# A diffusion-transformer block with a 16-expert MoE: both low parts of the first expert's w2 earlier on VectorE, w1's high parts laid out anew, overflow sums on GpSimd

## The reference

```python
h2 = rms_norm(x, norm2_g[layer]) * (1 + sc2) + sh2
...
scores = jax.nn.sigmoid(jnp.dot(h.astype(F32), router_w.astype(F32)))
biased = scores + router_b.astype(F32)
grp = biased.reshape(h.shape[0], N_EXPERT_GROUPS, EXPERTS_PER_GROUP)
grp_score = jnp.sum(lax.top_k(grp, TOP_K)[0], axis=-1)
best = jnp.argmax(grp_score, axis=-1)
...
for e in range(N_EXPERTS):
    he = jax.nn.silu(h @ w1[e]) * (h @ w3[e])
    y = y + gates[:, e:e + 1] * (he @ w2[e]).astype(F32)
...
x = x + g2 * f[:b * n].reshape(b, n, d)
...
return rms_norm(x, final_g)
```

## Time and profile before

| | us |
|---|---|
| median of 3 runs | 578.73 (577.07 to 579.29) |
| the profiled execution | 576.75 |
| its span | 574.2 |
| TensorE busy | 540.2 (94%) |
| VectorE busy | 445.2 (78%) |
| ScalarE busy | 322.2 (56%) |
| GpSimd busy | 159.4 (28%) |

### The profile page before, as it was taken

How to read it: one execution, slowest core, us unless ns; L and a number is a source line. 1 busy time by engine, 2 the same in 40 slices (tenths; PEclk the granted TensorE clock), 3 DMA queues, 4 the chain that set the end, 5 groups by cost and what they waited for, 6 DMA issues and landing times.

```text
span 574.2 us, 7711 instructions
## 1 busy us (share of the span) xinstructions
PE 540.2 (94%) x2747; PEld 411.3 (72%) x2747; DVE 445.2 (78%) x589; ACT 322.2 (56%) x398; POOL 159.4 (28%) x158
## 2 busy tenths in 40 slices
PE   1789999999998999989998999999999999999995
PEld 1344884677876778776786888888888888877772
DVE  1347686435667766488999999999999999999867
ACT  4540133345555742247566769667687676866624
POOL 6000843173134100013670332123330233300070
PEclk9899999999999999999999999999999999999998
DMA  8999997669520551169989999999999999999665
GB/s 292 390 372 318 372 379 282 195 179 403 224 73 3 199 205 50 62 214 391 340 318 391 393 382 389 391 392 393 392 391 387 389 393 387 364 381 348 197 235 204
DMA packets 88518, 173.13 MB, mean 302 GB/s; under 512 B 5399, under 2 KB 18907, under 8 KB 88365
## 3 DMA queue, kind: packets, MB, share of 16 engines
q1 hardware_dynamic: 82338, 154.65, 74.9%
q10 hardware_dynamic: 2780, 9.99, 4.3%
q0 software_dynamic: 3376, 8.18, 3.9%
HBM read 159.37 MB, written 17.33 MB: 308 GB/s over the span
## 4 chain that ended last, share of the span: by engine, by line
PE 76%; DVE 10%; DMA 6%; ACT 3%; issue 3%; SPq 1%; DVEq 0%; ACTq 0%
PE psum L941 6%; PE psum L1316 4%; PE psum L1318 4%; PE psum L1317 4%; PE psum L1343 4%; PE psum L1345 4%; PE psum L1344 4%; PE psum L1328 4%; PE psum L1327 4%; PE psum L1326 4%; PE psum L949 4%; DMA w<-in_moe_w 3%; DMA ada<-in_ada_w 3%; PE psum L990 3%; PE psum L992 3%
## 5 line engine op out<-in xcount | busy, mean ns | idle before, releaser
L2326 DVE TENSOR_TENSOR w_lo<-w,w_hi 128x2048 fp32r<-128x2048 f32 x32 | 72.9, 2280 | 1.2 <-ACT w_hi L1758 1.2
L2315 DVE TENSOR_TENSOR w_lo<-w,w_hi 128x1024 fp32r<-128x1024 f32 (+2 forms) x30 | 68.7, 2295 | 0.0
L1749 ACT CAST w_hi<-w 128x2048 fp32r<-128x2048 f32 x30 | 57.3, 1910 | 16.3 <-PE psum L1328 14.8
L1758 ACT CAST w_hi<-w 128x2048 fp32r<-128x2048 f32 x32 | 60.3, 1913 | 8.4 <-DVE ysb L2348 6.1
L2309 DVE TENSOR_TENSOR w_lo<-w,w_hi_a 128x2048 fp32r<-128x2048 f32 (+1 forms) x30 | 51.5, 1753 | 3.0 <-ACT w_hi_a L1737 1.8
L1343 PE MATMUL psum<-w_hi,heT_hi 128*128 128x512 f32 x120 | 49.6, 413 | 0.8 <-DVE w_lo L2326 0.8
L807 POOL COPY idx<-idx 128x1 int32 x12 | 10.6, 885 | 139.8 <-PE psum L1289 139.8
L1345 PE MATMUL psum<-w_hi,heT_lo 128*128 128x512 f32 x120 | 47.0, 392 | 0.0
L1317 PE MATMUL psum<-w_lo,xgT_hi 128*128 128x512 f32 x120 | 46.8, 390 | 0.0
L1327 PE MATMUL psum<-w_lo,xgT_hi 128*128 128x512 f32 x120 | 46.7, 389 | 0.0
L1326 PE MATMUL psum<-w_hi,xgT_hi 128*128 128x512 f32 x120 | 46.7, 389 | 0.0
(11 more groups left out here) (390 smaller groups left out, 1258.0 us busy)
## 6 DMA issues: line engine op xcount, KB each, us to landing
w<-in_moe_w SPq DMA_DIRECT2D x32, 2048.0 KB, 13.4
w<-in_moe_w SPq DMA_DIRECT2D x32, 1024.0 KB, 13.6
ada<-in_ada_w SPq DMA_DIRECT2D x12, 2048.0 KB, 18.3
win<-in_w_in SPq DMA_DIRECT2D x8, 1024.0 KB, 14.1
expert_rows<-ysb ACTq DMA_DIRECT2D x15, 512.0 KB, 6.3
expert_rows<-zero SPq DMA_DIRECT2D x1, 5120.0 KB, 20.0
wout<-in_w_out SPq DMA_DIRECT2D x4, 1024.0 KB, 5.2
x<-in_x SPq DMA_DIRECT2D x2, 1024.0 KB, 10.3
```

The source lines that it names most:

```text
L1758: act.copy(w2_hi[:, :, hs], w2_sb[b][:, :, hs]).then_inc(w2_hi_ok[half], 1)
L2315: v.tensor_tensor(w3_lo[b][:, ks, :], w3_sb[b][:, ks, :], w3_hi[:, ks, :], ALU.subtract).then_inc(w3_lo_ok, n)
L2326: v.tensor_tensor(w2_lo[b][:, :, hs], w2_sb[b][:, :, hs], w2_hi[:, :, hs], ALU.subtract).then_inc(w2_lo_ok[half], 1)
```

## The change

Four things, all in the stretch between the choice of experts and the second expert.

1. VectorE copies the counts out of PSUM into a new tile `counts` (semaphore `ranks_out`, which also takes over from `rmod_ok`), and GpSimd works out the block offsets of overflow from it, in 12 linked operations ahead of the first gather. VectorE's `overflow_blocks` loses that part and waits for the result (`tables_ok`, formerly `iota_ok`) ahead of `pick(off2)`.
2. `w1_hi_a` is laid out as three pairs of k; parts 0, 1, 2 lie at places 0, 2, 1, part 3 in `w1_hi_b` as before. Thereby ScalarE's first two casts of w1 for the second expert lie over G1 and SC2 and not over SH2.
3. ScalarE casts w1's parts 0 and 1 ahead of the first expert's turned rows (k = 0 to 7), and parts 2 and 3 ahead of k = 6, where parts 0 and 1 were.
4. On VectorE both halves of the first expert's `low_w2` stand behind w1's part 3 and ahead of `low_rows(1)`. `low_w1` is defined earlier, and its first call stands where it was in the order.

The core of the diff:

```diff
-        w1_hi_a = at("w1_hi_a", 144 * K1, [P, 6, FF], F32R)
+        w1_hi_a = at("w1_hi_a", 144 * K1, [P, 3, 2 * FF], F32R)
...
+        def w1_high(g, n=1):
+
+            if g == 3:
+                return w1_hi_b[:].rearrange("p (a k) f -> p a (k f)", a=1)
+            if n == 2:
+                assert g == 0
+                return w1_hi_a[:, 0:3:2, :]
+            place = (0, 2, 1)[g]
+            return w1_hi_a[:, place:place + 1, :]
...
             link(gp.memset(xg[1][:], 0.0))
 
+            gp.wait_ge(ranks_out, 1)
+            link(gp.tensor_scalar(off[:], counts[:], float(P + 1), None, ALU.is_ge))
+            for i, least in enumerate((2 * P + 1, 3 * P + 1)):
+                link(gp.tensor_scalar(ext[:], counts[:], float(least), None, ALU.is_ge))
+                link(gp.tensor_tensor((off[:], cs[:, 0, 8:])[i], off[:], ext[:], ALU.add))
+            for i, sh in enumerate((1, 2, 4, 8)):
+                a, b = cs[:, i % 2, :], cs[:, 1 - i % 2, :]
+                link(gp.tensor_tensor(b[:, 8:], a[:, 8:], a[:, 8 - sh:8 - sh + NE], ALU.add))
+                if i == 0:
+                    link(gp.tensor_scalar(counts[:], a[:, 8:], float(NE - 1), None, ALU.subtract))
+            link(gp.tensor_tensor(off[:], cs[:, 0, 8:], eno[:], ALU.subtract))
+            gp.tensor_tensor(off[:], off[:], counts[:], ALU.subtract).then_inc(tables_ok, 1)
+
             gp.wait_ge(idx_ok, 1)
...
             act.wait_ge(rwq_ok, 1)
+            act.wait_ge(w1_in[1], 16)
+            act.wait_ge(x1_ok, 2 * NT)
+            act.wait_ge(scale_ok, 2)
+            high_w1_part(1, 0)
+            high_w1_part(1, 1)
             for k in range(KD):
                 if k == 1:
                     store_h2(3)
                 if k == 6:
-                    act.wait_ge(w1_in[1], 16)
-                    high_w1_part(1, 0)
-                    high_w1_part(1, 1)
+                    high_w1_part(1, 2)
+                    high_w1_part(1, 3)
...
-            high_w1_part(1, 2)
-            high_w1_part(1, 3)
...
+            v.tensor_copy(counts[:], bank[7][:, NT * NE:(NT + 1) * NE]).then_inc(ranks_out, 1)
             pick(rank[:], bank[7][:, 0:NT * NE].rearrange("p (t e) -> p t e", e=NE).unsqueeze(2).to_broadcast(E2))
...
             index(0, NE, 1)
+            low_w1(1, 1, 0, 2)
...
-                above(cs[:, 0, 8:], bank[7][:, NT * NE:(NT + 1) * NE], [P + 1, 2 * P + 1, 3 * P + 1])
-                v.tensor_copy(ext[:], cs[:, 0, 8:])
-                for i, sh in enumerate((1, 2, 4, 8)):
-                    a, b = cs[:, i % 2, :], cs[:, 1 - i % 2, :]
-                    link(v.tensor_tensor(b[:, 8:], a[:, 8:], a[:, 8 - sh:8 - sh + NE], ALU.add))
-                run = cs[:, 0, 8:]
-
-                link(v.tensor_tensor(off[:], run, ext[:], ALU.subtract))
-                link(v.scalar_tensor_tensor(out=off[:], in0=off[:], scalar=float(NE - 1), in1=eno[:],
-                                            op0=ALU.add, op1=ALU.subtract))
+                v.wait_ge(tables_ok, 2)
                 pick(off2[:], off[:].unsqueeze(1).unsqueeze(1).to_broadcast(E2))
...
-            low_w1(1, 1, 0, 2)
             overflow_blocks()
             low_w1(1, 1, 2)
             low_w1(1, 1, 3)
+            low_w2(0, 0, 0)
+            low_w2(0, 0, 1)
             low_rows(1)
-            low_w2(0, 0, 0)
             gated(0)
...
             low_w3(1, 1, 2, 2)
-            low_w2(0, 0, 1)
             expert_rows(0, 0, 0, 0)
```

More of the change, by code:

```diff
@@ L258, in build @@
         ext = rt("ext", [P, NE])
+        counts = rt("counts", [P, NE])
         cs = rt("cs", [P, 2, 8 + NE])
@@ L318, in build @@
         bias_ok = sem("bias_ok")
-        iota_ok = sem("iota_ok")
+        tables_ok = sem("tables_ok")
         vecT_ok = sem("vecT_ok")
@@ L392, in build @@
         hot_ok = sem("hot_ok")
-        rmod_ok = sem("rmod_ok")
+        ranks_out = sem("ranks_out")
         idxps_ok = sem("idxps_ok")
@@ L785, in _ @@
             gp.iota(tok_chunk[:].rearrange("p (t k) -> p t k", k=2), [[1, NT], [0, 2]], base=-(EMPTY // P),
-                    channel_multiplier=0, allow_small_or_imprecise_dtypes=True).then_inc(iota_ok, 1)
+                    channel_multiplier=0, allow_small_or_imprecise_dtypes=True).then_inc(tables_ok, 1)
             gp.wait_ge(h2_stored[1], 16)
@@ L812, in _ @@
             gather_rows(1, idx[:, 1:2])
-            gp.wait_ge(rmod_ok, 1)
+            gp.wait_ge(ranks_out, 2)
             for i in range(NT * 2):
@@ L852, in _ @@
             gp.iota(iota_tok[:], [[1, N]], base=0, channel_multiplier=0, allow_small_or_imprecise_dtypes=True
-                    ).then_inc(iota_ok, 1)
+                    ).then_inc(tables_ok, 1)
             gp.wait_ge(ysb_free[0], n_pairs * 16 + 16)
@@ L1314, in hidden1 @@
                         pe.wait_ge(w1_lo_ok, s * 4 - (2 if k == 0 else 3 - k // 2))
-                    w_hi = w1_high(k)[:, 0, :]
+                    w_hi = w1_high(k // 2)[:, 0, (k % 2) * FF:(k % 2 + 1) * FF]
                     pe.matmul(bank[2][:], xgT_hi[:, k, :], w_hi, start=(k == 0), stop=False)
@@ L1736, in high_w1_part @@
             def high_w1_part(b, g):
-                act.copy(w1_high(2 * g, 2).rearrange("p k f -> p (k f)"),
+                act.copy(w1_high(g)[:, 0, :],
                          w1_sb[b][:, 2 * g:2 * g + 2, :].rearrange("p k f -> p (k f)")).then_inc(w1_hi_ok, 1)
@@ L2211, in _ @@
             v.wait_ge(prob_ok, 1)
-            v.wait_ge(iota_ok, 1)
+            v.wait_ge(tables_ok, 1)
             early_choice()
@@ L2260, in index, with low_w1 @@
                 v.tensor_copy(idx[:, b0:b1], idx_f[:, b0:b1]).then_inc(idx_ok, 1)
+            def low_w1(b, s, g, n=1):
+                v.wait_ge(w1_hi_ok, s * 4 - (4 - g - n))
+                ks = slice(2 * g, 2 * (g + n))
+                v.tensor_tensor(w1_lo[b][:, ks, :].rearrange("p (a k) f -> p a (k f)", a=n),
+                                w1_sb[b][:, ks, :].rearrange("p (a k) f -> p a (k f)", a=n), w1_high(g, n), ALU.subtract
+                                ).then_inc(w1_lo_ok, n)
             index(0, NE, 1)
+            low_w1(1, 1, 0, 2)
             def above(dst, src, limits):
@@ L2274, in overflow_blocks @@
                 v.scalar_tensor_tensor(out=rmod, in0=over[:], scalar=-float(P), in1=rank[:],
-                                       op0=ALU.mult, op1=ALU.add).then_inc(rmod_ok, 1)
+                                       op0=ALU.mult, op1=ALU.add).then_inc(ranks_out, 1)
                 pick(wsel[:], prob[:].unsqueeze(2).to_broadcast(E2))
@@ L2303, in overflow_blocks @@
                                 ).then_inc(hot_ok, 1)
[L2305 to L2310, removed]
             def low_w3(b, s, g, n=1):
@@ L2457, in _ @@
             low_w2(1, last, 1)
-            v.wait_ge(iota_ok, 2)
+            v.wait_ge(tables_ok, 3)
             link(v.tensor_copy(idx_last[:], idx1[1][:, 0:1]))
```

2 lines of the change are left out of this document (removed).

## The result

| | before | changed |
|---|---|---|
| median | 577.32 us (576.11 to 579.29, 6 runs) | 583.83 us (581.68 to 585.17, 6 runs) |
| the profiled execution | 576.75 | 582.99 |
| its span | 574.2 | 581.2 |

The changed kernel is slower: ratio 1.0105, 95% interval 1.0078 to 1.0132. The forecast was 581.2 against a median of 578.73, a ratio of 1.004; its range ended at 583.5, and the median of 583.83 lies just above that.

A forecast was written before the change was run, and what follows sets the result against it. TensorE, busy 540.2 of 574.2 us, was taken as the bound. Casts 0, sums and w2 move 0 on the path, copy 0.2 covered, `hot_mod` +2.5: 579.3 against the profiled 576.75, 581.2 against the median 578.73; range 577.0 to 583.5.

The forecast's parts named there:

- Where the wait is: TensorE at the overflow index product (L1280): waits for GpSimd's `hot_mod`, ending at 279.9, 2.5 us of idle.
- one matrix per VectorE operation: Rival at `hot_mod`: one matrix finishes at each change of VectorE's operation; L1280 waits 1.4 us, 580.1 us; chance 0.22.
- the forecast's rule: GpSimd's `hot_mod`: two changes of VectorE's operation for each held matrix, third at 273.1, fourth 277.5, then 0.6 us each.
- Sums not late: Overflow sums on GpSimd end near 267, VectorE needs them at about 267.9: no wait, by 0.9 us.
- copy covered: VectorE's copy of the counts ahead of `hot_slot` delays TensorE's index sums 0.2 us, covered by the `hot_mod` wait.
- casts and places free: ScalarE's earlier w1 casts add 0 on the path; the parts' new places change addresses alone, 2.29 us as before.
- slower by the sums being late: Rival at GpSimd's overflow sums: they end near 269.0, VectorE waits 1.1 us, TensorE loses 3.7: 582.4 us; chance 0.13.
- `hot_mod` +2.5: Term of the sum: TensorE's 2.5 us wait for GpSimd's `hot_mod` ahead of L1280, the only net cost on the path.
- nothing gives the 2.5 us back: Stretch after 279 and the loop: TensorE is the slow one there, so the 2.5 us lost stay lost.
- The faster rival: VectorE's relief reaches the gap at 315.15 and closes all of its 2.59 us: 576.1 us; chance 0.08.
- the gap at 315.15: TensorE's one real gap, at hidden_turned, 2.59 us idle, released by VectorE's `he`; forecast to stay as it is.

The follow-up runs named there:

- e5: Changed kernel with 12 unused 128x128 products on TensorE ahead of its wait for `hot_mod`; 580.86 us, ratio 1.0051.
- e1: Changed kernel with the old order of VectorE's two w2 low parts put back; 577.58 us, ratio 0.9994.
- e2: Kernel before with only the order of VectorE's two w2 low parts changed; 584.28 us, ratio 1.0105.
- e3: Changed kernel with 24 unused 128x128 products on TensorE ahead of its wait for `hot_mod`; 583.77 us, ratio 1.0099.
- e4: Changed kernel with `hot_mod` made by VectorE instead of GpSimd; 577.47 us, ratio 0.9985.
- e8: Changed kernel with three of the eight `hot_mod` matrices ahead of GpSimd's first gather; 580.62 us, ratio 1.0036.
- e6: Changed kernel with `hot_mod` on VectorE and three third-expert low parts moved forward around the second expert's `he`; 576.44 us, ratio 0.9975.
- e7: Kernel before with only three of the third expert's low parts moved forward around the second expert's `he`; 577.54 us, ratio 0.9988.
- e9: Changed kernel with `hot_mod` on VectorE, third-expert low parts moved forward, second w2 half behind the first `he`; 576.42 us, ratio 0.9969.

## Why the prediction was right in its mechanism and too small in its size

*Where the wait is: right.* It stands ahead of the overflow product, is released by `hot_mod`, and measured 2.66 us of idle where 2.5 were forecast. The end of the last matrix was put at 279.9 in the old kernel's time; it came at 279.34, which is 280.05 when the 0.71 us by which this profile is early are added. That `hot_mod` is held off by the operations from SBUF is right as well; how it is held is not. The forecast let two matrices through ahead of the long operations and had the next two each sit through one change of VectorE's operation.

*How near the 2.5 us came is in part luck.* One matrix was done before the long operations, not two, and of the three held ones only the third, 3.43 us long, sat through a change; the second and the fourth went at the next end of an operation, as the rival "one matrix per VectorE operation" had it. The two errors pull in opposite directions. From the second matrix's start at 269.37 and TensorE's readiness at 276.73 (279.39 - 2.66), I estimate that the forecast's rule would have given 3.2 us of idle (matrices done at 272.5 and 277.0, five more by 279.9), the rival's 2.1 (271.2, 272.5, 274.7, 277.0, three more by 278.8). The measured 2.66 lies between them. What decides whether a matrix sits through a change is open.

*Sums not late, copy covered, casts and places free: right.* The pair of low parts began at 262.68, the sums were done at 265.66, VectorE reached its wait at 266.8. VectorE did not wait, so *slower by the sums being late* fell.

*The step that failed* is the sum, and it is more than a detail: the text gave 0.64 to a change of at most 0.5% and 0.30 to slower than that, and the loss is 1.05%, over twice the 0.43% of the forecast. The sum ended with "`hot_mod` +2.5", and ahead of it stood "nothing gives the 2.5 us back", which looked only for something that would make the wait smaller. What TensorE does behind a gap was not asked; behind that of the earlier trace rows it had gone on at full clock. The missing term is the half clock: 3.23 us ahead of expert_out0 in the profile, 3 us by e5 against the changed kernel.

The second stretch, 1.48 us in the profile, is not the change's in the same sense: it follows a gap that both kernels have. Of the eight profiled executions with that gap at 2.57 to 2.60 us, it followed in six (the changed kernel, e1 to e4 and e8) and not in two (the kernel before and e5). e1, where it followed, is as fast as the kernel before by its median; so one profile's 1.5 us there say nothing on the change. The kernel before itself seems to have the stretch in many executions: of its 67 beside the experiments, 29 had a mean granted clock of 0.984 or 0.985 (median span 576.4 us) and 12 one of 0.990 or more (574.2), and its profiled one, with 0.991 and 574.2, is like the latter; where the clock fell in them is not on record. In e6, e7 and e9, where the later gap is closed, none of 34 was below 0.987. So a part of the 7.0 us between the two profiled spans is probably the choice of execution.

*The faster rival* was wrong as it stood and pointed at the right place: VectorE's relief did not reach the gap at 315.15 by itself (still 2.59 us), as the chain in the earlier trace rows said, but with three operations moved forward, two of them from behind the turned rows' low part to ahead of it, it did (e6); without the relief the same order only moved the wait to the `he` before (1.67 us, e7).

The Trainium skill (SBUF — State Buffer, "SBUF: two separate sides") has the pair of ports held for the whole instruction. If the operation that waits gets them at its end, the second and fourth matrix agree (they were done 0.4 and 0.5 us after it); the third, which began at 271.22, waited through VectorE's change of operation at 272.0 and ended at 274.65, does not.

## What to carry to other kernels

Ahead of moving long VectorE operations with two inputs in SBUF, look at what GpSimd runs at that time: eight operations, 0.6 us each when undisturbed, went from 6.1 us to 10.8 when the long ones came over them; small VectorE operations had been their cover, and ones that read PSUM left them at 0.6 as well. A gap on TensorE is to be priced with the half clock that may follow it, here 3 us for 2.7 us of idle; filler products in the gap are worth trying. An engine's relief was worth nothing here until the order let it shorten the chain that ends in a gap. And where the clock behind a gap falls in some executions and not in others, one execution of each kernel is not enough to compare them.

## What the runs showed that was not expected

- After an idle time of 2.63 us (e2) and 2.66 us (changed kernel), TensorE went on at a granted clock of 0.50, for 6.1 and 6.7 us; the clock had fallen within the gap. After one of 1.00 us (e8) it went on at 1.00 and fell to 0.50 only 1.4 us later. After the one of 2.59 us in the kernel before, and 1.67 us in e7, it stayed at 1.00. The same gap by `he` (2.57 to 2.60 us) gave both. What decides was not tried.
- The same eight matrices cost VectorE 1.81 us and would cost GpSimd, undisturbed, some 4.7 (an estimate, eight times the 0.59 of its last rows).
